# The last attention's head norms and rotations, made between the units of its query projection instead of after them

## The reference, cut to what matters

```python
def c_mixer(h_ctx, h_lat, w_in, q_norm_g, k_norm_g, w_out, need_ctx):
    def project(h):
        b, t, _ = h.shape
        q, k, v = jnp.split(h @ w_in, [C_WIDTH, C_WIDTH + C_KV_WIDTH], axis=-1)
        q = rms_norm_2(q.reshape(b, t, C_HEADS, C_HEAD_DIM), q_norm_g)
        k = rms_norm_2(k.reshape(b, t, C_KV_HEADS, C_HEAD_DIM), k_norm_g)
        return q, k, v.reshape(b, t, C_KV_HEADS, C_HEAD_DIM)
    ...
    q_l, k_l = apply_rope(q_l, cos, sin), apply_rope(k_l, cos, sin)
    ...
    o = lax.map(lambda qb: gqa_attend(qb, k_all, v_all), q_blocks)
```

## Time and profile before

| | us |
|---|---|
| median of 3 runs | 3340.22 (3336.49 to 3345.51) |
| the profiled execution's own time | 3337.52 |
| its span, first to last instruction | 3335.7 |
| PE busy | 3137.8 (94%) |
| DVE busy | 1599.4 (48%) |
| ACT busy | 1219.0 (37%) |

### The profile page before, as it was taken

One profiled execution on the slowest core, in us unless ns is written; L12 is line 12 of the kernel. 1 busy time (PEld: TensorE's weight loads), 2 busy tenths in 40 slices (PEclk: granted clock), 3 DMA queues, 4 the chain that ended last, 5 costly groups with the idle time before them and its releaser, 6 DMA issues. The chain is left out here.

```text
span 3335.7 us, 39122 instructions
## 1 busy us (share of the span) xinstructions
PE 3137.8 (94%) x15040; PEld 2458.7 (74%) x15040; DVE 1599.4 (48%) x2389; ACT 1219.0 (37%) x2029; POOL 141.5 (4%) x126
## 2 busy tenths in 40 slices
PE   7989999999898999998998998999999897899999
PEld 5666677763486677775885787788888775778887
DVE  4863666661254466665424633433333525343444
ACT  2543333332464333335213453422222424543332
POOL 2200000010000000001001101000000100010000
PEclk9969999999998999999998998999999999999999
DMA  5101443432301344341211000111111120022221
GB/s 188 52 26 38 177 176 117 173 104 37 89 1 51 126 154 174 123 153 33 64 39 51 1 1 26 65 62 61 65 55 71 51 76 1 1 76 101 101 87 64
DMA packets 157677, 259.15 MB, mean 78 GB/s; under 512 B 54332, under 2 KB 70074, under 8 KB 157436
## 3 DMA queue, kind: packets, MB, share of 16 engines
q1 hardware_dynamic: 155812, 252.66, 21.5%
q10 hardware_dynamic: 1628, 4.76, 0.4%
q0 software_dynamic: 128, 0.26, 0.0%
HBM read 255.57 MB, written 2.10 MB: 77 GB/s over the span
## 5 line engine op out<-in xcount | busy, mean ns | idle before, releaser
L1207 ACT ACTIVATE w_hi<-wbuf 128x1024 fp32r<-128x1024 f32 x330 | 348.4, 1058 | 1191.9 <-PE psA L756 1152.5
L754 PE MATMUL psA<-act_hi,w_hi 128*128 128x512 f32 (+1 forms) x1824 | 687.4, 377 | 57.9 <-DVE act_lo L1863 32.8
L755 PE MATMUL psA<-act_lo,w_hi 128*128 128x512 f32 (+1 forms) x1824 | 682.6, 374 | 0.0
L756 PE MATMUL psA<-act_hi,w_lo 128*128 128x512 f32 (+1 forms) x1824 | 681.4, 374 | 0.0
L1857 DVE TENSOR_TENSOR w_lo<-wbuf,w_hi 128x1024 fp32r<-128x1024 f32 x330 | 407.2, 1237 | 525.5 <-ACT w_hi L1207 520.3
L754 PE MATMUL psA<-hid_hi,w_hi 128*128 128x512 f32 (+1 forms) x1280 | 476.8, 373 | 5.5 <-DVE work L1966 4.6
L755 PE MATMUL psA<-hid_lo,w_hi 128*128 128x512 f32 (+1 forms) x1280 | 472.3, 369 | 0.0
L756 PE MATMUL psA<-hid_hi,w_lo 128*128 128x512 f32 (+1 forms) x1280 | 471.4, 368 | 0.0
L754 PEld LDWEIGHTS psA<-act_hi,w_hi 128*128 128x128 f32 x1824 | 349.5, 192 | 127.4 <-issue 47.3
L756 PEld LDWEIGHTS psA<-act_hi,w_lo 128*128 128x128 f32 x1824 | 348.5, 191 | 61.2
L755 PEld LDWEIGHTS psA<-act_lo,w_hi 128*128 128x128 f32 x1824 | 349.3, 192 | 58.6
(11 more groups left out here) (244 smaller groups left out, 3529.8 us busy)
## 6 DMA issues: line engine op xcount, KB each, us to landing
wbuf<-in_mlp_w_dram SPq DMA_DIRECT2D x64, 2048.0 KB, 8.2
work<-in_ada_w_dram SPq DMA_DIRECT2D x32, 1536.0 KB, 10.9
wbuf<-in_ab_w_in_dram SPq DMA_DIRECT2D x10, 1024.0 KB, 5.0
wbuf<-in_ple_w_gate_dram SPq DMA_DIRECT2D x4, 2048.0 KB, 8.3
wbuf<-in_hy_w_in_dram SPq DMA_DIRECT2D x3, 2048.0 KB, 13.8
wbuf<-in_c_w_in_dram SPq DMA_DIRECT2D x3, 2048.0 KB, 7.5
wbuf<-in_hy_w_out_dram SPq DMA_DIRECT2D x2, 2048.0 KB, 7.6
wbuf<-in_mla_w_out_dram SPq DMA_DIRECT2D x2, 2048.0 KB, 7.9
```

What stands on the lines that cost most here:

```text
L754: pe.matmul(psA[:, s, a:b], w_hi, x_hi[:, a:b], start=first, stop=False)
L755: pe.matmul(psA[:, s, a:b], w_hi, x_lo[:, a:b], start=False, stop=False)
L756: ins = pe.matmul(psA[:, s, a:b], w_lo, x_hi[:, a:b], start=False, stop=last)
L1207: return nc.scalar.activation(out, in_, func, **kw)
```

## The change

The stage `head_norms("c_n", ...)` and the meeting before it are removed (and with them the 20 entries of `PLAN_A`; one meeting less for POOL). In their place:

- The ten tiles have one order, `C_TILES`, with the two key tiles first: tile i is key head i for i = 0, 1 and query head i - 2 after that. The mean product of tile i is `c_norm(i)`, its rotation product `c_rotate(i)`. Both go to `psO`: the mean to columns 0 up to the tile's width, the rotation to columns 512 to 1023. So there is one place for a mean and one for a rotation, and new semaphores `c_mean`, `c_rot` and `c_rot_used` guard them.
- PE makes `c_norm(0)` ahead of unit 0, and after each unit u first `c_rotate(u - 1)` (for u of at least 1) and then `c_norm(u + 1)`. What is left comes after unit 7.
- ACT squares each tile right behind its copy, and takes `c_root(n - 4)` (Ln and Exp) at the end of the n-th turn of its loop.
- DVE makes `w_lo` of `c_q` 0 and 1 ahead of the copies of the values, and after each further `w_lo` of unit u makes `c_normalize(u - 2)` and, for u of at least 4, `c_turn(u - 4)`.
- Some areas of the working memory move (squares, roots, rotation's scratch, probabilities), so that they don't overlap the split activations still in use.

```diff
-          ("rms2", 1), ("c_k", 2), ("c_v", 2), ("c_q", 8), ("c_n", 20), ("cat", LT * C_H), ("c_out", 8),
+          ("rms2", 1), ("c_k", 2), ("c_v", 2), ("c_q", 8), ("cat", LT * C_H), ("c_out", 8),
...
+        C_TILES = [(8 + m, kC[:, m, :]) for m in range(C_KV)] + [(m, qC[:, m, :]) for m in range(C_H)]
...
         # PE
-            split_linear("c_q", sH[TOK], sL[TOK], LAT)
-            meet(pe)
-            head_norms("c_n", 6, 10, lambda m: qC[:, m, :] if m < 8 else kC[:, m - 8, :], sqc, C["mean128"], C["rot128"])
+            def c_norm(i):
+                w = C_TILES[i][1].shape[-1]
+                pe.wait_ge(S["head_sq"], 6 + i + 1)
+                if i >= 1:
+                    pe.wait_ge(S["root_set"], 6 + i)
+                for a, b in ((0, 512), (512, w)):
+                    if b > a:
+                        ins = pe.matmul(psO[:, a:b], C["mean128"], sqc[:, i % 4, a:b], start=True, stop=True)
+                ins.then_inc(S["c_mean"], 1)
+            def c_rotate(i):
+                pe.wait_ge(S["rope_raw"], 6 + i + 1)
+                if i < C_KV:
+                    pe.wait_ge(S["root_set"], 6 + C_KV)
+                if i >= 1:
+                    pe.wait_ge(S["c_rot_used"], i)
+                pe.matmul(psO[:, 512:512 + LAT], C["rot128"], C_TILES[i][1][:, 0:LAT], start=True, stop=True).then_inc(S["c_rot"], 1)
+            c_norm(0)
+            for u in range(C_H):
+                split_linear("c_q", sH[TOK], sL[TOK], LAT, None, u + 1, first=u)
+                if u >= 1:
+                    c_rotate(u - 1)
+                c_norm(u + 1)
+            c_rotate(7)
+            c_norm(9)
+            c_rotate(8)
+            c_rotate(9)
             meet(pe)
             attention("cat")
...
         # ACT
+            def c_root(i):
+                act.wait_ge(S["c_mean"], i + 1)
+                if i >= 2:
+                    act.wait_ge(S["rope_raw"], 6 + i - 1)
+                root = rsc[:, i % 2, 0:C_TILES[i][1].shape[-1]]
+                f(root, psO[:, 0:root.shape[-1]], ACT.Ln, bias=eps_rms)
+                act.drain()
+                f(root, root, ACT.Exp, scale=-0.5).then_inc(S["root_set"], 1)
             for n in range(len(c_units) + 2):
                 if 2 <= n < len(c_units):
                     w_hi(*c_units[n])
                 if n >= 2:
                     name, m = c_units[n - 2]
                     ps, free = get_a(act, name, m)
-                    dst = kC[:, m, :] if name == "c_k" else qC[:, m, :]
+                    dst = C_TILES[n - 2][1]
                     f(dst, ps[:, 0:dst.shape[-1]], ACT.Copy).then_inc(free, 1)
-            meet(act)
-            head_norms("c_n", 6, 10, lambda m: qC[:, m, :] if m < 8 else kC[:, m - 8, :], sqc, rsc)
+                    act.drain()
+                    f(sqc[:, (n - 2) % 4, 0:dst.shape[-1]], dst, ACT.Square).then_inc(S["head_sq"], 1)
+                if n >= 4:
+                    c_root(n - 4)
+            c_root(8)
+            c_root(9)
...
         # DVE
+            w_lo("c_q", 0)
+            w_lo("c_q", 1)
             for g in range(2):
                 ...
-            for u in range(8):
+            def c_normalize(i):
+                m, x = C_TILES[i]
+                v.wait_ge(S["root_set"], 6 + i + 1)
+                stt(x, x, cq8 if m < 8 else vec("ck", 0), rsc[:, i % 2, 0:x.shape[-1]], ALU.mult, ALU.mult).then_inc(S["rope_raw"], 1)
+            def c_turn(i):
+                x = C_TILES[i][1][:, 0:LAT]
+                v.wait_ge(S["c_rot"], i + 1)
+                tt(rtc[:, i % 2, :], psO[:, 512:512 + LAT], C["sinC"], ALU.mult).then_inc(S["c_rot_used"], 1)
+                tt(x, x, C["cosC"], ALU.mult)
+                v.drain()
+                tt(x, x, rtc[:, i % 2, :], ALU.add)
+            for u in range(2, 8):
                 w_lo("c_q", u)
-            meet(v)
-            head_norms("c_n", ...)
+                c_normalize(u - 2)
+                if u >= 4:
+                    c_turn(u - 4)
+            for i in range(6, 10):
+                c_normalize(i)
+                c_turn(i - 2)
+            c_turn(8)
+            c_turn(9)
             meet(v)
...
-BEFORE_MLP3 = 2
+BEFORE_MLP3 = 1
```

More of the change, by code:

```diff
@@ L248, in build @@
         qC, vC, kC = area(KD, LAT, at=3 * KD * TOK), area(6, 256, at=4 * KD * TOK), area(C_KV, TOK, at=0)
-        sqc, rsc, rtc = area(4, TOK), area(2, TOK), area(2, LAT)
-        prob3, turn3 = area(2, TOK), area(2, TOK)
+        sqc, rsc = area(4, TOK), area(2, TOK)
+        assert cursor[0] <= KD * TOK
+        rtc = area(2, LAT, at=3 * KD * TOK + KD * LAT)
+        prob3, turn3 = area(2, TOK, at=KD * TOK), area(2, TOK)
         on3 = area(LT, D, at=3 * KD * LAT)
@@ L266, in build @@
         S = {n: sem(n) for n in (
-            "centered", "squared", "sum_ready", "sum_read", "mean_read", "acc_set", "acc_mean", "ple_set", "tile_sum", "norm_set", "acc_zero", "relu_used", "gate_used", "act_hi", "act_split", "w_hi", "w_split", "g_hi", "hidden_set",
+            "centered", "squared", "sum_ready", "sum_read", "mean_read", "acc_set", "acc_mean", "ple_set", "tile_sum", "c_mean", "c_rot", "c_rot_used", "norm_set", "acc_zero", "relu_used", "gate_used", "act_hi", "act_split", "w_hi", "w_split", "g_hi", "hidden_set",
             "ada_used", "ada_sum", "row_ready", "row_set", "row_turned", "conv_set", "vec_set", "sqrt_set", "lam_exp", "lam_set",
@@ L2418, in _ @@
                                       ps[:, 0:256 * n].rearrange("p (t c) -> p t c", c=256)).then_inc(free, 1)
-            for u in range(8):
-                w_lo("c_q", u)
-            meet(v)
-            head_norms("c_n", 6, 10, lambda m: qC[:, m, :] if m < 8 else kC[:, m - 8, :], rsc, rtc,
-                       lambda m: cq8 if m < 8 else vec("ck", 0), C["cosC"], C["sinC"])
+            def c_normalize(i):
[10 more added lines that the diff above has]
+            for u in range(2, 8):
+                w_lo("c_q", u)
+                c_normalize(u - 2)
[6 more added lines that the diff above has]
+            c_turn(9)
             meet(v)
```

## The result

| | before | after |
|---|---|---|
| median | 3342.86 us (4 runs, 3336.49 to 3348.95) | 3379.38 us (4 runs, 3378.26 to 3381.55) |
| span of the profiled execution | 3335.7 | 3376.8 |
| values' end to the first logits | 86.6 | 128.0 |

The ratio is 1.011, with a 95% interval of 1.0089 to 1.0131: slower by 1.1%, clear of the noise. The profiled spans differ by 41.1 us and the stretch of the change by 128.0 - 86.6 = 41.4, so the whole difference lies in this stretch. The 86.6 runs from 2701.84, the end of the values, to 2788.47; the 128.0 from 2701.74, `c_norm(0)`, to the first logits at 2829.76.

The account below looks back on a forecast made before the run. It took the head norms as wholly on the path, partly waiting. Gaps and tail at full clock (+24.3), units' clock (+11.9) and tail's clock (+4) gave +40.2; it said 3379 us, range 3360 to 3392.

Parts of the forecast that it names:

- The stage and the gap removed: Head norms and meeting go, 39.2 us, with PE's 1.8 us gap before unit 0 and about 2 of clock behind it.
- The wait at each unit: After units 0 to 6 PE waits for ACT's root or DVE's turn; seven gaps of 4.3 to 5.4, 34.6 us together.
- Full clock, +24.3: Without clock losses, attention would begin at 2812.7 in place of 2788.4, 24.3 us later.
- The tail at full clock: From unit 7's end to attention, remaining products and exchanges run with nothing beside them, taking 19.7 us.
- The clock: PE runs slower behind gaps: seven times 1.7, 11.9 us (0 to 20.7), plus 4 in the tail (0 to 5.2).
- The hidden case: Rival: roots made during the units leave no gaps between them; -15 us, 3322 to 3325, chance 0.04.
- What would show it: Profile signs: PE gaps of 4 to 5.5 us, ended twice by ACT then DVE; periods 12 to 14; stretch near 125.
- The bounds of +30 to +48: The slowdown in us that the main forecast, chance 0.60, was said to span with its own bounds.

Follow-up runs that it names:

- the part alone: Kernel before, with DVE making the low parts of the first two query units' weights ahead of the values' copies; 3336.74 us, 0.9991 of before.
- the tail filled: Changed kernel with dummy f32 products of constants on PE in its seven gaps between units and the tail's four gaps; 3362.5 us.
- ACT's order alone: Changed kernel with ACT taking the root at the start of its turn, ahead of `w_hi`'s wait for the unit; 3351.42 us, 1.0035 of before.
- filled gaps: Changed kernel with four dummy f32 products of constants on PE after each of units 0 to 6, no wait changed; 3370.09 us.
- DVE's order alone: Changed kernel with DVE making each turn ahead of the weights' low part and the next norm; 3358.51 us, 1.0055 of before.
- both orders: Changed kernel with ACT's root ahead of `w_hi` and DVE's turn ahead of the low part and next norm; 3318.97 us, 0.9943 of before.

## Why the prediction was right

The forecast was 3379 with 3360 to 3392, and 3379.38 came. Point by point:

- *The stage and the gap removed, 39.2 + 1.8 + 2.* Right: the part alone took 3.8 us off the units. 0.9 of it came back in the head norms, a stage that the whole change removes.
- *The wait at each unit.* Predicted were 4.3, 4.3, 5.4 four times, and 4.4, from the moment PE could go on; the trace has 4.20, 4.20, 5.16 four times and 4.15 of idle time, counted from the modelled end of the last matmul, some 0.2 later. Who ends them was right too, and the two reorderings show both causes: each takes away its own wait and leaves the other.
- *Full clock, +24.3.* The measured 41.4 less the clock's 12.9 and 4.3 is 24.2.
- *The tail at full clock, 19.7 from the end of unit 7.* With the tail filled, 4.3 and 15.1, thus 19.4.
- *The clock, 11.9 for seven gaps and 4 for the tail.* Measured 12.9 and 4.3. That the sum came so near is partly luck. Four gaps of the same 5.16 us lost between 1.4 and 2.9 each, and four of 3.82 us in the kernel with ACT's order alone lost 2.6 to 3.0 each. So the length of a gap does not give its cost, and 1.7 was right as a mean only. The Trainium skill's rule (TensorE: Matmul & The Clock Gate, section HAM oscillation), that such a loss is paid at every wait, held for these seven gaps: each period is longer than with filled gaps. It did not hold for the gaps of 2.90 us, two of which cost nothing.
- *The hidden case, -15.* The prediction ruled it out by ACT's wait alone, and held that roots made beside the units would leave no gaps. That was half of it: with the root first, four gaps of 3.82 us stayed, for DVE's order. With both waits moved the stretch came to 67.3, thus -19.3. The units took what was predicted (56.6 us); the tail took 10.8 in place of 15. The 15 has the turns behind the norms: with that order and filled gaps it is 15.1 us from the rotation after unit 7 to the first logits.
- *What would show it.* The gaps and who ends them came as said. The periods reached 15.5 us, where 12 to 14 were forecast, by the clock behind one gap, and the stretch 128.0, where it was near 125.

The bounds of +30 to +48 given there are narrower than the prediction's own terms, which allow 24.3 to 50.2; the stated range covers these too. The predicted sum for the profiled execution was 3377.7, and that execution took 3378.64. The medians differ less (36.5) than the stretches (41.4). That the sum added to the median before (3380.4) came so near is partly chance, since before varies by some 12 us over its runs.

## What to carry to other kernels

Whether a stage hides beside another was decided here by what stood ahead of each piece in its engine's queue, not by the room on the engine. Write down for each piece when its input is ready and which wait it is queued behind; if that wait is for the very work it should run beside, move the piece ahead of it. Do this for every engine in the chain: either move alone still left 11 to 18 us lost against before, and only both together turned 36 us lost into 21 us won. And count gaps on PE twice, since each of 3.8 us or more in this stretch also cost 1.4 to 3 us of clock behind it. Shorter ones sometimes did too.

## What the runs showed of the hardware

What a gap on PE costs in clock did not follow its length:

| gap, us | where | clock lost behind it, us |
|---|---|---|
| 1.90 | DVE's order alone, behind unit 6 | nothing |
| 1.92 | before, ahead of unit 0 | 1.8 |
| 2.90 (four) | DVE's order alone | nothing twice, 1.6 and 1.5 |
| 3.82 (four) | ACT's order alone | 2.6 to 3.0 |
| 4.15 to 5.16 (seven) | the changed kernel | 1.4 to 2.9 |

Gaps of the same 5.16 us cost unlike amounts: the stretch of 14.0 us had a mean clock of 0.88, that of 15.5 us, with the same instructions, 0.78. The runs do not show why. Products of constants into a bank that nobody reads kept the clock at 1.00 through gaps and gave back 17 of 128 us without a wait being changed. The order of the queues was worth more: with every gap filled the stretch was 110.8 us, with both orders 67.3.
